# Block 1 of a two-block transformer kernel: finer first pieces, heads' means and roots by row tile on GpSimd, meta keys' products by halves of the heads, last norms in halves

## The reference, cut to what matters

```python
h = rms_norm(x, attn_norm_g); qa, ka, va, qb, kb, vb = split(h @ w_in)
# kind a: 8 query heads, 2 key heads of 64; kind b: 4 pairs of heads of 64, values of 128
q, k = rope(rms_norm(head, g)) for every head          # a mean and a root per head and row
out_a = softmax(qa ka^T / 8) va
out_b = rms_norm((softmax(q0 k0^T / 8) - lam * softmax(q1 k1^T / 8)) vb) * (1 - lam_init)
x = x + concat(out_a, out_b) @ w_out
x = x + (silu(n @ w_gate) * (n @ w_up)) @ w_down       # n = rms_norm(x)
```

```python
h = h + rms_norm(mix_out, norm_mix_post)
h = h + rms_norm(mlp_out, norm_mlp_post)
```

## Time and profile before

| what | value |
|---|---|
| median of 3 runs | 765.17 us |
| profiled execution | 766.98 us |
| its span | 765.7 us |
| TensorE busy | 745.6 us (97%) |
| VectorE, ScalarE, GpSimd busy | 460.6, 373.7, 100.7 us |
| HBM read | 128.62 MB, 169 GB/s over the span |
| block 1 up to its FFN | 0 to about 136 us |

### The profile page before, as it was taken

How to read it: one execution, slowest core, us unless ns; L and a number is a source line. 1 busy time by engine, 2 the same in 40 slices (tenths; PEclk the granted TensorE clock), 3 DMA queues, 4 the chain that set the end, 5 groups by cost and what they waited for, 6 DMA issues and landing times.

```text
span 765.7 us, 11055 instructions
## 1 busy us (share of the span) xinstructions
PE 745.6 (97%) x4406; PEld 645.2 (84%) x4406; DVE 460.6 (60%) x653; ACT 373.7 (49%) x535; POOL 100.7 (13%) x120
## 2 busy tenths in 40 slices
PE   5999999999999999999999999999999999999996
PEld 3877778999999999888888888888778899988895
DVE  5887766675555555455747665675847743555433
ACT  6566654654444444275443543564437644344431
POOL 1763603100000000000110000000302111011110
PEclk9999999999999999999999999999999999999999
DMA  8542413677666566537445643474536766655511
GB/s 307 199 140 83 138 31 113 213 248 241 203 213 181 181 202 215 161 111 247 141 135 182 195 137 91 138 234 134 198 95 203 245 212 193 195 189 189 179 47 55
DMA packets 70163, 130.46 MB, mean 170 GB/s; under 512 B 5296, under 2 KB 29056, under 8 KB 70112
## 3 DMA queue, kind: packets, MB, share of 16 engines
q1 hardware_dynamic: 68352, 125.45, 51.7%
q0 software_dynamic: 1552, 4.20, 1.6%
q10 hardware_dynamic: 208, 0.10, 0.0%
HBM read 128.62 MB, written 1.05 MB: 169 GB/s over the span
## 4 chain that ended last, share of the span: by engine, by line
PE 93%; DVE 3%; DMA 2%; ACT 1%; issue 1%; SPq 0%; DVEq 0%; ACTq 0%
PE psum L428 41%; PE psum L850 27%; PE psum L469 12%; PE psum L892 2%; PE psum L645 1%; PE psum L977 1%; PE psum L564 1%; PE psum L509 1%; PE psum L594 1%; DMA w_raw<-in_w_in 1%; PE psum L1009 1%; PE psum L545 1%; DVE w_lo L1856 1%; DMA w_raw<-in_w_down 1%; PE psum L620 1%
## 5 line engine op out<-in xcount | busy, mean ns | idle before, releaser
L1856 DVE TENSOR_TENSOR w_lo<-w_raw,w_hi 128x1024 fp32r<-128x1024 f32 x225 | 275.9, 1238 | 151.8 <-ACT w_hi L1235 151.1
L1235 ACT ACTIVATE w_hi<-w_raw 128x1024 fp32r<-128x1024 f32 x231 | 241.3, 1059 | 178.2 <-PE psum L850 78.3
L850 PE MATMUL psum<-h_hi,w_hi 128*128 128x256 f32 x608 | 170.1, 284 | 0.8 <-issue 0.6
L850 PE MATMUL psum<-h_hi,w_lo 128*128 128x256 f32 x608 | 169.7, 283 | 0.0
L850 PE MATMUL psum<-h_lo,w_hi 128*128 128x256 f32 x608 | 162.1, 282 | 0.0
L850 PEld LDWEIGHTS psum<-h_hi,w_hi 128*128 128x128 f32 x608 | 114.8, 189 | 2.4 <-issue 0.7
L850 PEld LDWEIGHTS psum<-h_hi,w_lo 128*128 128x128 f32 x608 | 114.5, 188 | 0.0
L850 PEld LDWEIGHTS psum<-h_lo,w_hi 128*128 128x128 f32 x608 | 111.0, 189 | 0.6
L428 PE MATMUL psum<-w_hi,h_hi 128*128 128x512 f32 (+1 forms) x256 | 102.3, 399 | 9.2 <-DVE h_lo L1960 9.2
L428 PE MATMUL psum<-w_hi,h_lo 128*128 128x512 f32 (+1 forms) x256 | 100.7, 393 | 0.0
L428 PE MATMUL psum<-w_lo,h_hi 128*128 128x512 f32 (+1 forms) x256 | 100.6, 393 | 0.0
(11 more groups left out here) (298 smaller groups left out, 972.1 us busy)
## 6 DMA issues: line engine op xcount, KB each, us to landing
w_raw<-in_w_in SPq DMA_DIRECT2D x78, 512.0 KB, 4.6
w_raw<-in_w_down SPq DMA_DIRECT2D x54, 512.0 KB, 4.3
w_raw<-in_w_up SPq DMA_DIRECT2D x32, 512.0 KB, 4.2
w_raw<-in_w_gate SPq DMA_DIRECT2D x44, 256.0 KB, 2.9
w_raw<-in_w_up SPq DMA_DIRECT2D x44, 256.0 KB, 3.2
w_raw<-in_w_out SPq DMA_DIRECT2D x16, 512.0 KB, 3.7
w_raw<-in_w_branch_a SPq DMA_DIRECT2D x4, 512.0 KB, 4.3
w_raw<-in_w_branch_b SPq DMA_DIRECT2D x4, 512.0 KB, 5.1
```

The lines of the kernel that those rows point to most:

```text
L850: mm = pe.matmul(outs, x[:, cols], y[:, kc, :], start=kc == 0 and n == 0, stop=kc == KC - 1 and n == (1 if i == 0 else 2))
L1235: act.activation(T.w_hi[:, k % SLOTS, :], T.w_raw[:, k % RAW_SLOTS, :], ACT.Copy).then_inc(S.w_rounded, 1)
L1856: dve.tensor_tensor(T.w_lo[:, k % SLOTS, :], T.w_raw[:, k % RAW_SLOTS, :], T.w_hi[:, k % SLOTS, :], ALU.subtract).then_inc(S.w_cut, 1)
```

## The change

Transfers: fill 0 is sent as two halves, the first ahead of all else; the first transposed pair goes on ScalarE's queue in the place of the meta tokens and their tables, which move to SyncE's queue behind the small ones; `vectors` (512 KB: tables, gains) goes ahead of fill 4, with a semaphore of its own; the last output DMA goes on ScalarE's queue. Slab qa is made by `first_chunk`, in the order hi by hi, hi by lo, lo by hi for both tiles, each with its own wait. `head_sum` only sums; `head_root` on GpSimd takes one tile: mean, power, row scale. The zero products are gone, the first product of unit 0 starts the bank. The meta unit is four products of half the rows by half the columns, the last two behind a wait of TensorE for its first two. In the post norms the squares are scaled by 1/sqrt(D), the mean is one operation, and the last norm scales both tiles' first halves first. GpSimd's list has `clear_blocks("b")` early, `blocks_a` behind `meta_kb`, `cut(19)` and `cut(21)` behind `blocks_b`, `root_b` last. Pieces of qb, kb, vb, oa and ob, units and scores change places on TensorE, and the lists of ScalarE and VectorE with them.

```diff
@@ sync_program
+    sp.dma_start(T.w_raw[:, 0:1, 0:WIDE], W.half).then_inc(S.half_landed, 16)
     for k, pieces in enumerate(W.fills):
-        if k < KC // 2:
+        if 0 < k < KC // 2:
             sp.dma_start(T.xt[:, 2 * k:2 * k + 2, :], ...)
+        if k == RAW_SLOTS:
+            sp.dma_start(T.vectors[:], a["vectors"]).then_inc(S.vectors_landed, 16)
         if k == RAW_SLOTS + 2:
             sp.dma_start(T.small[:], a["small"]).then_inc(S.small_landed, 16)
-            sp.dma_start(T.vectors[:], a["vectors"]).then_inc(S.small_landed, 16)
+            sp.dma_start(T.xm[:], a["meta_tokens"]).then_inc(S.meta_landed, 16)
+            sp.dma_start(T.rope1m[:], a["rope1m"]).then_inc(S.small_meta_landed, 16)
@@ tensor_program
+    def first_chunk(kc):
+        k, c = kc // 2, kc % 2
+        w_hi, w_lo = w(T.w_hi, k, c, 2), w(T.w_lo, k, c, 2)
+        for n, (x, y) in enumerate(((T.h_hi, w_hi), (T.h_hi, w_lo), (T.h_lo, w_hi))):
+            if n == 0:
+                pe.wait_ge(S.first_rounded, kc + 1)
+                pe.wait_ge(*((S.half_rounded, 1) if kc == 0 else (S.w_rounded, k + 1)))
+            elif n == 1:
+                pe.wait_ge(*((S.half_cut, 1) if kc == 0 else W.cut(S, k)))
+            else:
+                pe.wait_ge(S.first_cut, kc + 1)
+            for t in range(TILES):
+                mm = pe.matmul(bank[t][:], x[:, kc, t * P:(t + 1) * P], y, ...)
@@ attend_unit
-            open_sums("a")
...
-                mm = pe.matmul(sums[:], T.pTm[kind][:, t * P:(t + 1) * P], T.vmD[kind][:], start=False, stop=True)
+            rows = META * (A_HEADS if kind == "a" else B_HEADS) // 2
+            for n, (half, t) in enumerate(((0, 0), (1, 1), (0, 1), (1, 0))):
+                if n == 2:
+                    pe.wait_ge(S.meta_weighed, 1 if kind == "a" else 2)
+                part, cols = slice(half * rows, (half + 1) * rows), slice(half * WIDE // 2, (half + 1) * WIDE // 2)
+                mm = pe.matmul(bank[SUMS[kind][t]][:, cols], T.pTm[kind][part, t * P:(t + 1) * P], T.vmD[kind][part, cols],
+                               start=False, stop=n >= 2)
+                if n == 1:
+                    mm.then_inc(S.meta_weighed, 1)
@@ TensorE's list
-    slab("qa", KC, ((0,), (1,)), first=True)
+    for kc in range(KC):
+        first_chunk(kc)
     slab("kva", KC, ((2,), (3,)), meta=7)
     piece("qb", 0, 0)
+    piece("qb", 0, 1)
     piece("qb", 1, 0)
-    piece("qb", 0, 1)
     piece("qb", 0, 2)
+    piece("qb", 1, 1)
     turn_qa(0)
     turn_qa(1)
...
@@ scalar_program
-    act.dma_start(T.xm[:], a["meta_tokens"]).then_inc(S.meta_landed, 16)
-    act.dma_start(T.rope1m[:], a["rope1m"]).then_inc(S.small_meta_landed, 16)
+    act.dma_start(T.xt[:, 0:2, :], a["turned"][:, 0:2, :]).then_inc(S.turned_landed[0], 16)
+    round_half(0)
     round_first(0)
-    round_half(0)
+    round_half(1)
     round_first(1)
-    round_half(1)
-    round_fill(1)
     round_first(2)
     round_first(3)
+    round_fill(1)
@@ scalar_program, end
-    for t in range(TILES):
-        for half in range(2):
-            post_square(1, t, half, ..., rows_scale(3, t))
+    for half in range(2):
+        for t in range(TILES):
+            post_square(1, t, half, ..., T.stat[:, 8 + t:9 + t])
+    act.wait_ge(S.x_posted, 8)
+    act.dma_start(rows_of(out)[1][:, :, WIDE:D], T.x[:, 1, WIDE:D]).then_inc(S.stored[1], 16)
@@ vector_program
     cut_first(0)
+    cut_first(1)
     cut_fill(1)
-    cut_first(1)
     cut_first(2)
+    scale_meta()
     cut_first(3)
...
-        ss, n = T.stat[:, 4 + 2 * t:6 + 2 * t], 4 * place + 2 * t
-        step(dve.tensor_tensor(ss[:, 0:1], ss[:, 0:1], ss[:, 1:2], ALU.add))
-        own()
-        dve.tensor_scalar(ss[:, 0:1], ss[:, 0:1], 1.0 / D, EPS, ALU.mult, ALU.add).then_inc(S.post_mean, 1)
+        dve.tensor_scalar(T.stat[:, 4 + 2 * t:5 + 2 * t], T.stat[:, 4 + 2 * t:5 + 2 * t], T.stat[:, 5 + 2 * t:6 + 2 * t], EPS,
+                          ALU.add, ALU.add).then_inc(S.post_mean, 1)
...
+    post_scale(1, 0, 0, 4, T.bg[1], scale[0])
+    post_scale(1, 1, 0, 6, T.bg[1], scale[1])
+    post_mean(1, 0)
+    post_scale(1, 0, 1, 5, T.bg[1], scale[0])
+    post_add(1, 0, HALVES)
+    post_mean(1, 1)
+    post_scale(1, 1, 1, 7, T.bg[1], scale[1])
+    post_add(1, 1, HALVES)
@@ pool_program
+        pool.wait_ge(S.rope_summed, ROPE_BEFORE[name] + t + 1)
+        step(pool.tensor_scalar(ss, ss, scale, bias, ALU.mult, ALU.add))
+        own()
...
         step(root(ss))
         own()
         pool.wait_ge(S.x_root, 1)
-        pool.tensor_tensor(by_tile, by_tile, T.row_scale[:, 0, :].unsqueeze(2).broadcast_to([P, TILES, heads]),
-                           ALU.mult).then_inc(S.rope_root, 1)
+        pool.tensor_tensor(ss, ss, T.row_scale[:, 0, t:t + 1].broadcast_to([P, heads]), ALU.mult).then_inc(S.rope_root, 1)
     rows_table("qa")
-    root_meta()
     rows_table("ka")
     root_x()
+    rows_table("qb")
+    root_meta()
     clear_blocks("a")
-    rows_table("qb")
     rows_table("kb")
-    head_root("qa")
-    head_root("ka")
+    head_root("qa", 0)
+    head_root("qa", 1)
+    head_root("ka", 0)
+    head_root("ka", 1)
     meta_ka()
+    clear_blocks("b")
+    head_root("qb", 0)
+    head_root("qb", 1)
+    head_root("kb", 0)
+    head_root("kb", 1)
+    meta_kb()
     blocks_a()
-    head_root("qb")
-    head_root("kb")
-    meta_kb()
+    blocks_b()
     cut(19)
     cut(21)
-    clear_blocks("b")
-    blocks_b()
-    root_b()
     cut(23)
     cut(25)
+    root_b()
```

More of the change, by code:

```diff
@@ L187, in slab @@
             rows = src[j * per * P:(j + 1) * per * P, :].rearrange("(c p) n -> p c n", p=P)
+            if not self.fills:
+                self.half = rows[:, 0:1, :]
+                self.fills.append([(lambda raw: raw.rearrange("p (c n) -> p c n", c=2)[:, 1:2, :], rows[:, 1:2, :])])
+                continue
             self.fills.append([(lambda raw, per=per: raw.rearrange("p (c n) -> p c n", c=per), rows)])
@@ L406, in sync_program @@
     for t in range(TILES):
-        for half in range(2):
+        for half in range(2 - t):
             cols = slice(half * WIDE, (half + 1) * WIDE)
@@ L430, in chunk, with slab @@
         return mm
-    def slab(name, chunks, outs, x_hi=T.h_hi, x_lo=T.h_lo, ready=None, meta=None, between=None,
-             first=False):
+    def slab(name, chunks, outs, x_hi=T.h_hi, x_lo=T.h_lo, ready=None, meta=None, between=None):
         per = W.per[name]
@@ L597, in scores @@
                     mm.then_inc(S.scored, 1)
-    def open_sums(kind):
-        for b in SUMS[kind]:
-            pe.matmul(bank[b][:], T.zero[:], T.qT["a"][:, 0:2, :], start=True, stop=False)
     def turn_unit(u):
@@ L751, in tensor_program @@
     turn_kbm()
-    attend_unit(5)
+    piece("vb", 0, 3)
     turn_unit(6)
@@ L2205, in vector_program @@
     rows_qb(0)
+    cut_qa(0)
+    cut_fill(11)
+    rows_qb(1)
     cut_qa(1)
```

441 lines of the change are left out of this document (215 added, 226 removed).

## The result

The changed kernel takes **760.79 us** (median of 4 runs, 760.27 to 761.36), the kernel before 765.27 us (4 runs, 764.82 to 765.60): 4.5 us less by the medians. The ratio on record is 0.9934, with a 95% interval from 0.9921 to 0.9947, which is 4.1 to 6.0 us less. The prediction was 758.8 us, 756.4 to 762.3. The changed kernel, timed again later (experiment 9), took 760.87 us (0.9940, 0.9923 to 0.9957). The kernel before, run 56 times over all comparisons here, lies between 764.4 and 767.9 us, median 765.75.

What follows compares the result with a forecast made beforehand. TensorE was taken to bound the kernel, VectorE second. Terms 4.0 + 1.1 + 1.2 + 0.5 + 0.2 - 0.6 = 6.4 us, off the 765.17 us median, gave 758.8 us; 8 in 10: 756.4 to 762.3 us.

Steps and rivals of the forecast that it cites:

- Base: Whole kernel: gains summed against the profiled execution, 766.98 us, and subtracted from the median, 765.17 us.
- Start of slab qa: Block 1's start: first matmul at 5.8 us, slab over at 20.4 instead of 24.55; gain 4.0 us.
- Heads' chain on GpSimd: Head norms of qa, qb, kb: mean, power, product at 3.2 us per row tile, +2.8 us for each.
- The five turns: TensorE's transposes of the heads' rows: five margins of 0 to 1 us where there were 1.2 to 3.
- Rivals 1 and 4: 1: heads' chain decides, not TensorE, 761.3 us, chance 0.25. 4: full cascade of late chains, 767.2 us, chance 0.05.
- New stalls: TensorE's waits for the heads' chain in block 1: 0.6 us lost in sum, from -0.5 to +3.5.
- Zero products: The two products opening the sums, 0.57 us twice, go without a substitute: gain 1.1 us.
- meta products: Meta keys' products, kinds a and b: half-row products run side by side, 1.25 us each; gain 1.2 us.
- rival 3: Meta keys' products: the halves don't run together or drain; 1.5 us less gain, 760.3 us, chance 0.10.
- Last norms: Kernel's end: first half scaled earlier, mean in one operation; gain 0.5 us, 0.2 to 0.6.
- middle norm: Middle post norm: one 0.19 us operation leaves the chain of TensorE's 1.8 us wait; gain 0.2 us.
- Nothing after FFN 1 changes.: From FFN 1's start, 6 us earlier, nothing changes but 0.2 us in the middle norm.

Runs made afterwards that it cites:

- experiment 9: The changed kernel, unchanged, timed and profiled again: 760.87 us, ratio to the kernel before 0.9940.
- run 56: Not a label but a count ("run 56 times"): the kernel before, unchanged, over all comparisons: 764.4 to 767.9 us, median 765.75.
- second profile of before: The kernel before, unchanged, timed and profiled once more: median 766.25 us, profiled execution 765.77 us, ratio 1.0012 to its own copy.
- experiment 12: The changed kernel with GpSimd's cut of fill 19 moved ahead of the DMA issues of blocks_b, timed again in five rounds: 759.14 us.
- experiment 7: The changed kernel with the first turned pair on SyncE's queue, between the two half slabs, instead of ScalarE's queue: 761.48 us.
- experiment 10: The changed kernel with cut 19 ahead of blocks_b and the heads' mean, power and product made for both row tiles at once: 761.12 us.
- experiment 6: The changed kernel with the vectors loaded behind fill 5, as before the change, instead of ahead of fill 4: 760.97 us.
- Experiment 4: The changed kernel with both pairs of zero products and the two full meta products of 512 columns put back: 762.38 us.
- experiment 2: The changed kernel with each chunk of slab qa waiting for all its parts ahead of its first matmul: 762.01 us.
- experiment 5: The kernel before with h_lo of chunk 1 ahead of the cut of fill 1 in VectorE's list: 765.79 us, ratio 0.9998.
- experiment 8: The changed kernel with cut 19 ahead of blocks_b and slab qa's last h_lo ahead of VectorE's meta piece: 759.19 us.
- experiment 11: The changed kernel with cut 19 ahead of blocks_b and the vectors sent ahead of fill 5 instead of fill 4: 759.87 us.
- experiment 3: The changed kernel with GpSimd's cut of fill 19 moved from behind the DMA issues of blocks_b to ahead of them: 759.23 us.

## Why the prediction was right, step by step

The time, 2.0 us above the forecast, lies inside the range: a gain of 4.5 us by the medians, where 6.4 were forecast. Where it comes from is seen between the second profile of before (span 764.5) and the profile after (759.5): slab qa's end 22.50 to 20.37, **2.1**; from there to FFN 1's first matmul 126.48 to 123.29, **3.2**; from it to the last matmul 608.95 to 609.60, **-0.65**; behind it 6.57 to 6.24, **0.3**; 5.0 in sum. Part of the hit is luck: the start was priced 1.9 us too high, and 1.6 us that was not in the sum at all (below, "What this lets go") nearly made up for it.

- **Base.** I made the sum against a profiled execution that I knew to be 1.8 us above the median, and took the gain from the median. Such an excess isn't spread evenly: this execution was late in slab qa, the very stretch that the change shortens, and its stop and late change to the 2.4 GHz pace went into the 4.0 us. This is the step that failed most.
- **Start of slab qa, 4.0.** The end was right: first matmul 6.08 (5.1 to 6.05 given, 5.8 taken), slab over at 20.37 (20.4 predicted), held by the last h_lo as forecast. That the numbers agree to 0.03 us is luck: two more profiles of the same start (experiments 9 and 12) have 20.68 and 20.22. Against the usual start of before, 22.50, it is worth 2.1. The Trainium skill (DMA: Bandwidth & Descriptors, Issuing engines are not separate DMA queues) had the pair at its worst end; the trace agrees, it landed at 5.52; and experiment 7 is in line with it: on SyncE's queue, with fewer bytes ahead, it was there before 4.4.
- **What this lets go.** Not in my sum, since the late execution had no such wait: with a usual start the kernel before waits 1.5 us at turn_kam, where the meta keys are ready at 44.13. In the changed kernel they are ready at 43.05, and more pieces of qb and kb stand ahead of the turn, so TensorE comes at 43.31 and doesn't wait. That is 1.6 us, and without it much of the fast slab would be waited away, as the two profiles of before show (2.08 us sooner at the slab's end, 0.63 at FFN 1). With the 1.1 and 0.95 us of the products and 0.7 us of small stalls that are gone, less the 1.29 at scores(14), it makes 3.1 of the 3.2 us of this stretch. The split of the roots and the early vectors are no further gains: they are what keeps the chain on time, 1.6 us of it by experiment 10 and at most 0.8 by experiment 6.
- **Heads' chain on GpSimd.** Forecast 3.2 us a tile, from 2.58 for 8 columns. Measured 2.2 to 2.9 in five of six tiles and 3.5 in one: the power is 1.63 to 1.66 in all 8-column rows of the changed kernel. The five turns hold, as forecast, without a stall (I had 0.0 to 0.4 at turn_ka). Rivals 1 and 4 had no case. The 2.58 was no price of a power of 8 columns. Beside it in the trace of before stands a cut of VectorE that began just ahead. The changed kernel has a mean behind such a cut, and experiment 10 one ahead of it:
```profile
116.85 1.22 DVE L1856 TENSOR_TENSOR w_lo<-w_raw,w_hi 128x1024 fp32r<-128x1024 f32 x1
```
```profile
45.07 1.21 DVE L1893 TENSOR_TENSOR w_lo<-w_raw,w_hi 128x1024 fp32r<-128x1024 f32 x1
45.24 1.10 POOL L2808 TENSOR_SCALAR head_square_sums<-head_square_sums 128x8 f32<-128x8 f32 x1 [1.72 <-DVE head_square_sums L1932]
```
```profile
40.60 0.18 POOL L2809 TENSOR_SCALAR head_square_sums<-head_square_sums 16x2 f32<-16x2 f32 x1
...
40.90 1.23 DVE L1893 TENSOR_TENSOR w_lo<-w_raw,w_hi 128x1024 fp32r<-128x1024 f32 x1
```
The cut of before ends at 118.07 us and the power 1.53 us later, about its usual length. The mean at 45.24 ends at 46.34, the cut at 46.28. The meta keys' mean takes 0.18 us in experiment 10, where the cut begins behind it, and 1.22 us in the changed kernel (at 40.23), where a cut begins at 40.19 and ends at 41.40. Each long mean of the changed kernel (0.69, 0.90, 1.10, 1.22 and 1.84 us) ends 0.05 to 0.06 us behind such an operation of VectorE with two operands in SBUF. So VectorE's cuts hold up GpSimd, as GpSimd's cuts hold up VectorE below; a power that has begun isn't slowed by a cut that begins behind it (1.65 us at 27.57 us, with a cut from 28.81). No run here was made to test this; it is read from the traces.
- **New stalls, 0.6.** 1.29 us, in one place that no step of mine named: scores(14), through the two cuts that I had followed only to their due times in oa ("covered"). Two small stalls of before (0.2 us at 53.3, 0.5 at 102.9, by the second profile) are gone in return.
- **Zero products, 1.1, meta products, 1.2.** The first I take from the earlier trace rows, 0.57 us twice, since no run prices it alone; the second is 1.41 and 1.40 us in place of 1.87 and 1.91, so 0.95. The halves run side by side; kind b, in tiles of 32 rows, costs as much as kind a, so rival 3 is out: the rule on changes of tiling mode (the Trainium skill, TensorEngine Tiling (Array Packing), Key Properties) speaks of a drain, and no more than 0.2 us shows at either end of the step. Experiment 4 finds 1.3 of the 2.1 us between slab and FFN 1.
- **Last norms, 0.5, middle norm, 0.2.** From the last matmul's start to the start of the last additions 2.23 us instead of 2.64, 0.4; from there to the end of the span 4.0 instead of 3.9. The middle wait is 1.6 instead of 1.8 us.
- **"Nothing after FFN 1 changes."** Against the second profile of before 0.65 us was lost there (the first profile of before needs 609.54 us for the same stretch, as much as the changed kernel, but loses it in FFN 1). Here it is lost at 551 us, where TensorE waits for VectorE, whose addition stands behind the cut of a fill that landed late:
```profile
547.30 1.06 ACT L1270 ACTIVATE w_hi<-w_raw 128x1024 fp32r<-128x1024 f32 x1 [2.38 <-DMA w_raw<-in_w_out]
...
551.00 0.50 PE L503 MATMUL psum<-w_hi,h_hi 128*128 128x512 f32 x1 [0.51 <-DVE tmp L2528]
```
The stall (0.4 to 0.9 us) is in the profiles of after and of experiments 2 and 4 to 12, experiment 5's among them (0.47 us), which has nothing of the change there, and not in the two of before nor in experiment 3, while experiment 12, the same kernel, has it. It varies between executions, so the 0.65 us can't be put down to the change; that the change makes it more frequent isn't ruled out.

**The stall at scores(14) by the trace.** VectorE's operation of two columns, with two operands in SBUF, stands still as long as GpSimd cuts, while a product out of PSUM and a reciprocal with a single operand, at 92.36 and 92.96 us, ran beside the same cuts at their usual length (0.68, 0.16). The kernel before has it too, there with a copy inside SBUF, without harm:
```profile
82.94 2.35 POOL L2742 TENSOR_TENSOR w_lo<-w_raw,w_hi 128x1024 fp32r<-128x1024 f32 x1
...
83.32 2.06 DVE L2082 COPY squares<-maps 128x128 f32<-128x128 f32 x1
...
85.44 0.21 DVE L2082 COPY squares<-maps 128x128 f32<-128x128 f32 x1
```
The change had put both cuts behind each other and behind blocks_b, so one hold became 3.47 us, at a place where a bank of scores hung on the maxima queued behind it. The Trainium skill says it (SBUF — State Buffer, two separate sides): VectorE and GpSimd share a port pair that is an exclusive lock for a whole instruction, for VectorE's operations with two SBUF inputs or in a two-port mode. Here the trace agrees, with 3.47 us against 0.22, and further: GpSimd's second cut, which began at about 94.2, came ahead of the waiting operation. Why the waiting operation wasn't served between the two was not tried. Experiment 3 is the test of this reading: with one cut in the place of two, the operation ends with that one cut.

## What to carry to other kernels

Take a second profile of the kernel before, if there is one, and measure a gain from the stage as it usually runs; what one long execution has too much may sit just where you look for gain. A faster stage pays only up to the next chain that did not move: read what that chain's end is (here GpSimd, at 43.2 and 43.4 us in the two profiles) before you count. And when work is moved on GpSimd, look not only at who waits for its result but at VectorE beside it: its operations with two SBUF inputs stand while GpSimd's long cuts run (3.47 us for 0.22), two such cuts in a row count as one, and GpSimd's short operations stand in the same way behind VectorE's cuts (1.10 us for 0.20). A price that is read off one row may contain such a hold: look at what the other engine did at that moment.
